# V rows of three token blocks: read in table order and multiplied with matrices of one-hot products, instead of gathered

## What is computed

```python
def block(xblk):                                   # 128 tokens
    q = (xblk @ w_q).reshape(PEER_BLOCK, PEER_HEADS, 2, PEER_HALF)
    s = jnp.einsum('thcd,hcnd->thcn', q, sub_keys).astype(jnp.float32)
    sv, si = lax.top_k(s, PEER_TOPK)
    ...
    expert = jnp.take_along_axis(cidx, pos, axis=-1)          # 8 heads x 16 of 16384 experts per token
    g = jax.nn.softmax(top_s, axis=-1)
    u = u_table[expert]
    hid = jax.nn.gelu(jnp.einsum('thkd,td->thk', u, xblk).astype(jnp.float32), approximate=False)
    v = v_table[expert]
    return jnp.einsum('thk,thkd->td', (g * hid).astype(xblk.dtype), v)
```

## Time and profile before

| | us |
|---|---|
| three runs, median (lowest to highest) | 3677.02 (3660.54 to 3686.26) |
| profiled execution | 3657.85 |
| its span, first to last instruction | 3655.7 |

### The profile page before, as it was taken

The page is one execution under the profiler, slowest core; times in us unless marked ns, Lnnn a source line. Parts: engine busy times, 40 slices in busy tenths (PEclk is TensorE's granted clock), DMA queues, the critical chain, the costliest instruction groups (busy, mean ns, idle before and its releaser), DMA issues.

```text
span 3655.7 us, 27703 instructions
## 1 busy us (share of the span) xinstructions
PE 1964.2 (54%) x9448; PEld 1078.6 (30%) x9448; DVE 2036.2 (56%) x4571; ACT 323.3 (9%) x778; POOL 2092.7 (57%) x2183
## 2 busy tenths in 40 slices
PE   6975553765763348655833367566633233333446
PEld 6765431543540125333601034233301000000001
DVE  2379747567548773664377843654586744443220
ACT  2211011011100010110100011101000000000000
POOL 0045523656557675566466765665576666666665
PEclk9985786976886669767866579678855655656569
DMA  6587965998999999999999999999999999999998
GB/s 224 179 308 282 398 224 184 385 398 342 387 396 360 364 358 394 402 351 401 340 388 361 356 375 394 396 363 395 358 359 368 359 374 366 367 371 376 372 371 324
DMA packets 442170, 1286.15 MB, mean 352 GB/s; under 512 B 39408, under 2 KB 157936, under 8 KB 442032
## 3 DMA queue, kind: packets, MB, share of 16 engines
q0 software_dynamic: 313344, 1140.99, 81.9%
q1 hardware_dynamic: 126224, 134.48, 11.0%
q10 hardware_dynamic: 2464, 8.91, 0.6%
HBM read 1274.50 MB, written 9.44 MB: 351 GB/s over the span
## 4 chain that ended last, share of the span: by engine, by line
POOL 24%; PE 17%; DMA 17%; issue 16%; DVE 15%; another core or an unknown queue 9%; ACT 1%; SPq 0%; POOLq 0%; ACTq 0%; DVEq 0%
POOL ring L631 24%; PE ps L1257 11%; DMA ring<-in_peer_v_dram,v_idx 9%; DVE ring L899 6%; PE ps L1216 4%; DMA ring<-in_peer_u_dram,u_idx 4%; DVE work L976 2%; DMA wbuf<-in_peer_w_q_dram 2%; DMA wbuf<-in_w_in_dram 1%; DVE work L972 1%; PE ps L1224 1%; DVE work L981 1%; DVE work L1073 1%; PE ps L1415 0%
## 5 line engine op out<-in xcount | busy, mean ns | idle before, releaser
L899 DVE CUSTOM_DVE_ANT_0 ring<-ring,ps 128x1024 f32<-128x1024 f32 x1088 | 1300.3, 1217 | 943.9 <-DMA ring<-in_peer_u_dram,u_idx 798.5
L631 POOL DMA_INDIRECT ring<-in_peer_u_dram,u_idx x1088 | 1037.7, 954 | 991.8 <-issue 275.7
L1216 PE MATMUL ps<-ring,spread 128*32 128x512 f32 x4352 | 874.5, 906 | 1231.0 <-DMA ring<-in_peer_v_dram,v_idx 1080.0
L631 POOL DMA_INDIRECT ring<-in_peer_v_dram,v_idx x1088 | 1053.2, 968 | 552.1 <-issue 303.5
L1257 PE MATMUL ps<-wbuf,actT 128*128 128x256 f32 (+1 forms) x2944 | 708.2, 400 | 111.6 <-issue 75.8
L1216 PEld LDWEIGHTS ps<-ring,spread 128*32 128x32 f32 x4352 | 177.8, 143 | 1821.8 <-issue 1759.8
L1257 PEld LDWEIGHTS ps<-wbuf,actT 128*128 128x128 f32 (+1 forms) x2944 | 560.2, 194 | 282.0 <-issue 182.3
L972 DVE MAX8 work<-work 128x8 f32<-128x128 f32 (+3 forms) x432 | 109.8, 322 | 60.0 <-ACT work L868 56.8
L976 DVE FIND_INDEX8 work<-work 128x8 uint32<-128x128 f32 (+3 forms) x432 | 134.0, 329 | 6.7 <-issue 6.7
L701 ACT COPY spread<-weightT 128x16 f32<-128x16 f32 x64 | 14.0, 219 | 878.3 <-remote 654.1
L899 DVE DVE_READ_ACCUMULATOR2_ANT hidden<- 128x1 f32 x1088 | 88.9, 82 | 0.0
(11 more groups left out here) (153 smaller groups left out, 1271.2 us busy)
## 6 DMA issues: line engine op xcount, KB each, us to landing
wbuf<-in_w_in_dram SPq DMA_DIRECT2D x55, 1024.0 KB
wbuf<-in_peer_w_q_dram SPq DMA_DIRECT2D x40, 1024.0 KB
wbuf<-in_w_out_dram SPq DMA_DIRECT2D x20, 1024.0 KB
ring<-in_peer_u_dram,u_idx POOLq DMA_INDIRECT x1088
ring<-in_peer_v_dram,v_idx POOLq DMA_INDIRECT x1088
x_v<-x_scratch ACTq DMA_DIRECT2D x8, 512.0 KB
out_dram<-x_v ACTq DMA_DIRECT2D x8, 512.0 KB
x_in<-in_x_prompt_dram SPq DMA_DIRECT2D x7, 512.0 KB
```

Of the source, the lines that this page charges most:

```text
L631: pool.indirect_dma_start(ring[:, at % RING, :], None, table, bass.IndirectOffsetOnAxis(ap=idx, axis=0)).then_inc(landed[at % RING], 16)
L899: ch.put(v_.tensor_tensor_reduce(out=row, in0=row, in1=ux_ps, scale=1.0, scalar=0.0, op0=ALU.mult, op1=ALU.add, accum_out=hidden[:, k:k + ...
L1216: mm = pe.matmul(ps[j:j + 32, B_ACC + c, :], spread[:, at:at + 32], tile[:, 512 * c:512 * c + 512], start=(t % 32 == 0), stop=(t % 32 == 3 ...
```

## The change

- `DENSE = [3, 4, 5]`: the V rows of these blocks are no longer gathered. 384 gathers of 512 KB leave the phases 2, 3 and 4, and `PHASES` cuts the remaining V work anew, so that block 1's ends in phase 3 and block 2's in phase 4. Phase 5 keeps its 192 u and 320 v.
- In phase 5, V is read once in table order: 128 tiles ("dense"), each 2 x 512 columns of 128 x 2 rows, 512 KB, by plain DMAs from SP into the same ring. An expert's number is 128 i1 + i2. The tiles go through four sessions (half of the i2 values, half of the columns).
- For each half of i2, a matrix `denseW` (128 i1 values x 64 i2 values x 384 tokens) is built ahead of its sessions: for four tokens at a time ("group", 96 per half), DVE writes one-hot rows of i1 (one `tensor_tensor` of 512) and of i2 times the weight (four `tensor_scalar` of 64), PE multiplies them (four matmuls of 64 columns), ACT copies the product out. Two buffers each.
- A dense tile then takes six matmuls of 128 x 128 by 512 columns (2 values of i2, 3 blocks). Sessions end in a copy or an addition of three 128 x 512 sums ("spill"), and blocks 3, 4 and 5 get their final norm after the last dense tile.
- `beside` spreads the dense items over phase 5's list: about 0.94 gathers after each build group, about 2.3 after each dense tile. After the last dense tile 35 v items of the sample are left.
- The ring has 13 places instead of 14; `weightT` has six buffers; the mixing stage's buffers share one tensor with `denseW`. The `x1` load of a final norm is its own item.

The order of items gives these numbers of gathers per stretch (u+v, by `Pace`; "rest" of a phase counted with `peer`):

| stretch | phase 2 before | phases 3, 4 before | phases 2, 3 after | phase 4 after |
|---|---|---|---|---|
| first norm and `w_in` | 54+24 | 48+40 | 48+20 | 39+16 |
| attention and retention | 66+32 | 55+56 | 53+28 | 43+24 |
| `w_out` and second norm | 20+13 | 25+32 | 27+16 | 46+24 |
| `w_q` | 24+26 | 23+16 | 20+8 | 0+0 |
| `peer` and rest | 92+97 | 105+112 | 108+56 | 128+0 |

In phase 5 after: build of half 0 with 48+43 gathers, sessions 0 and 1 with 75+73, build of half 1 with 34+56, sessions 2 and 3 with 35+84 and 29 of the sample, then 35 of the sample.

The core of the diff:

```diff
-RING = 14
+RING = 13
+DENSE = [3, 4, 5]
...
-    ([3, 4], [(1, 0, 64, 128), (2, 1)]),
-    ([5, 6], [(3, 2), (4, 3)]),
-    ([7, 8], [(5, 4), (6, 5)]),
+    ([3, 4], [(1, 0, 64, 128), (2, 1, 0, 64)]),
+    ([5, 6], [(3, 1, 64, 128), (4, 2, 0, 64)]),
+    ([7, 8], [(5, 2, 64, 128), (6, None)]),
...
+SESSIONS = [(0, 0), (0, 1), (1, 1), (1, 0)]
...
+    for n, (half, _) in enumerate(SESSIONS):
+        if n % 2 == 0:
+            items += [(0, ("oh", half, g)) for g in range(2)]
+            for g in range(GROUPS):
+                items.append((1.0, ("build", half, g)))
+                if g + 2 < GROUPS:
+                    items.append((0, ("oh", half, g + 2)))
+        items += [(2.45, ("dense", n, i)) for i in range(PAIRS)]
...
+                    sp.dma_start(ring[:, at % RING, :].rearrange("p (a n) -> p a n", a=2),
+                                 v_pairs[:, half * PAIRS + i, :, 512 * cols:512 * cols + 512]
+                                 ).then_inc(landing(at), 16)
...
+                act.wait_ge(built, n + 1)
+                src = ps[:, B_W[n % 2], 0:GROUP * I2].rearrange("p (t i) -> p i t", t=GROUP)
+                ch.put(copy(denseW[:, :, GROUP * g:GROUP * g + GROUP], src), w_copied)
...
+                if n >= 2:
+                    dve.wait_ge(built, n - 1)
+                t0, shape = GROUP * g, [P, GROUP, P]
+                ch.put(v_.tensor_tensor(one1[:, n % 2], iota.unsqueeze(1).broadcast_to(shape),
+                                        digit[:, 0, t0:t0 + GROUP].unsqueeze(2).broadcast_to(shape), ALU.is_equal))
+                for i in range(GROUP):
+                    t = t0 + i
+                    w = weightT[:, DENSE[t // P] % WTBUF, t % P:t % P + 1]
+                    ch.put(v_.tensor_scalar(one2[:, n % 2, i, :], iota[:, I2 * half:I2 * half + I2],
+                                            digit[:, 1, t:t + 1], w, ALU.is_equal, ALU.mult),
+                           ones_ready if i == GROUP - 1 else None)
...
+                for i in range(GROUP):
+                    mm = pe.matmul(ps[:, B_W[n % 2], i * I2:i * I2 + I2], one1[:, n % 2, i, :], one2[:, n % 2, i, :],
+                                   start=True, stop=True)
+                mm.then_inc(built, 1)
...
+                tile = await_tile(pe, "d", n * PAIRS + i)
+                for a in range(2):
+                    for j in range(len(DENSE)):
+                        mm = pe.matmul(ps[:, j, :], denseW[:, 2 * i + a, P * j:P * j + P],
+                                       tile[:, 512 * a:512 * a + 512], start=(i == 0 and a == 0),
+                                       stop=(i == PAIRS - 1 and a == 1))
```

More of the change, by code:

```diff
@@ L81, in u_before @@
     return SLOTS * b
+DENSE = [3, 4, 5]
+V_AT = {b: i for i, b in enumerate(b for b in range(NBLK) if b not in DENSE)}
 def v_before(b):
-    return P * b
+    return P * V_AT[b]
 def v_token(b, i):
@@ L161, in seg_items, with dense_items, beside @@
     return items
+GROUP = 4
+GROUPS = P * len(DENSE) // GROUP
+I2 = NKEY // 2
+PAIRS = I2 // 2
+SESSIONS = [(0, 0), (0, 1), (1, 1), (1, 0)]
+DENSE_SLOTS = PAIRS * len(SESSIONS)
+def dense_items():
+    items = [(0, ("digits", 0, 0))]
+    for n, (half, _) in enumerate(SESSIONS):
[6 more added lines that the diff above has]
+        items += [(2.45, ("dense", n, i)) for i in range(PAIRS)]
+        if n < 3:
+            items.append((0, ("spill", n, 0)))
+    for b in DENSE:
+        items += [(0, ("x1", b, 0)), (0, ("final", b, 0))]
+    return items
+def beside(items, others):
+    share = 0.93 * sum(kind in "uv" for kind, _, _ in items) / sum(n for n, _ in others)
+    out, seen, due, at = [], 0, 0.0, 0
+    for item in items:
+        while at < len(others) and due <= seen:
+            out.append(others[at][1])
+            due += others[at][0] * share
+            at += 1
+        out.append(item)
+        seen += item[0] in "uv"
+    return out + [item for _, item in others[at:]]
 def plan():
@@ L173, in plan @@
         out.append(items)
-    out[-1].append(("final", prev[1], 0))
+    out[-1] = beside(out[-1], dense_items()) + [("final", prev[1], 0)]
     return out
 PLAN = plan()
+ENDS = [b for items in PLAN for kind, b, _ in items if kind == "final"]
+assert ENDS == [b for items in PLAN for kind, b, _ in items if kind == "x1"] and len(ENDS) == NBLK
+END_AT = {b: n for n, b in enumerate(ENDS)}
 def gather_order():
@@ L188, in gather_order @@
                 order["v", v_before(b) + k] = len(order)
+            elif kind == "dense":
+                order["d", b * PAIRS + k] = len(order)
     return order
@@ L404, in hymba_peer_program @@
         landed = [sem(f"landed{i}") for i in range(RING)]
+        landed_d = [sem(f"landed_d{i}") for i in range(RING)]
         y_stored = sem("y_stored")
@@ L699, in spread_out @@
                 if v != SAMPLE:
-                    src = weightT[:].rearrange("p (j r) -> p r j", j=groups)[:, piece * runs:(piece + 1) * runs, :]
+                    src = weightT[:, v % WTBUF, :].rearrange("p (j r) -> p r j", j=groups)[:, piece * runs:(piece + 1) * runs, :]
                     ch.put(copy(dst, src), spread_ready)
@@ L888, in item @@
                     weights(b)
+                elif kind == "digits":
+                    digits()
+                elif kind == "spill" and b == 2:
+                    dve.wait_ge(dense_done, PAIRS * 3)
+                    dve.wait_ge(spilled, 2 * len(DENSE))
+                    for j in range(len(DENSE)):
+                        half = dense_sum[:, j, 512:1024]
+                        ch.put(v_.tensor_tensor(half, half, ps[:, j, :], ALU.add), spilled)
+                elif kind == "oh":
+                    one_hot(b, k)
                 elif kind == "final":
@@ L1200, in item @@
                     quad(b, k // QUAD)
+                elif kind == "build":
+                    build(b * GROUPS + k)
+                elif kind == "dense":
+                    dense(b, k)
                 elif kind == "weights":
```

193 lines of the change are left out of this document (137 added, 56 removed).

## The result

The change made the kernel slower: 3902.52 us in the median of four runs (3897.36 to 3907.49), against 3668.79 for the kernel before (four runs); the ratio is 1.062 with a 95% interval of 1.059 to 1.066. The profiled execution took 3897.73 us, its span 3895.3, and the forecast on that basis was 3715: 183 us too little. The forecast's direction held, its range (3640 to 3850) did not.

The account below looks back on a forecast made before the run. Transfers were taken to bound the kernel from 636 us on, PE the sessions after the change. 3657.85 - 387 (phases 2 to 4) + 444 (phase 5) = 3715 us, 3734 on the median; range 3640 to 3850.

Parts of the forecast that it names:

- Sessions: Phase 5, dense tiles: PE takes over as the bound at its full clock, 775 us, against 595 of transfers.
- Rival 2: Phase 5 sessions: long matmuls go faster, sessions at the transfers' 595 us, program 3554 us on the median; chance 0.05.
- Tail: End of phase 5: three chained final norms, then the sample's last strip, norm and store, 62 us (50 to 80).
- the change of phase: Phase 5: the change of phase, plus weights and final norms ACT must do between build copies, 8 us.
- Builds: Phase 5, building `denseW`: 1.85 us per group, 1.75 in half 1, 346 us together (300 to 425).
- the price of `tensor_scalar`: Builds, DVE: each of four 64-element operations per group taken at 0.12 us, so 1.09 per group with the 512-element one.
- the clock: Builds, PE: a PE busy 66% of its time had a clock of 0.80, used for the 1.85 us per group.
- Rival 3: Phase 5: PE's clock is low, builds 67 us more, sessions some 75; 3850 us on the median; chance 0.15.
- Phases 2 to 4: Removing 384 gathers (528 us of transfers) shortens these phases by 70, 173 and 144 us, together -387.
- attention: Attention stage of phases 2 and 3: 118 us each, between 111 of transfers and 125, from a chain over three engines.
- Rival 4: Phases 2 to 4: held by chains over all engines, only -300 us; 3821 on the median; chance 0.1.
- rival 1: Phases 2 to 4: give all their bare sums allow, -461 us; 3660 on the median, no change; chance 0.25.

Follow-up runs that it names:

- e8: Changed kernel with four instead of six matmuls per dense tile (block 5's sum left incomplete): 3534.83 us, ratio 1.037 to the kernel before.
- e6: Changed kernel with all gathers, dot products and quads moved from beside the builds to beside the sessions: 3668.74 us, ratio 1.076 to the kernel before.
- e15: Changed kernel with U and V tiles of phase 5 taken one by one in turn, not in bunches of four: 3717.95 us, ratio 1.090.
- e12: Changed kernel with one-hot rows from two 256-element operations and an unused 256-column matmul per build group: 3715.2 us, ratio 1.088.
- e16: Changed kernel with U and V in turn, one-hot rows from two 256-element operations, and an unused 256-column matmul per build group: 3665.37 us, ratio 1.075.
- e7: Changed kernel with DVE placing its dot products a quarter into each `peer` step, not a tenth: 3736.7 us, ratio 1.096 to the kernel before.
- e9: Changed kernel with two dense blocks instead of three, block 3's V rows gathered again: 3710.09 us, ratio 1.013 to the kernel before.
- a0: Changed kernel with three dense blocks, unaltered, run again as an anchor: 3885.13 us, ratio 1.060 to the kernel before.
- e10: Changed kernel with two dense blocks, only V gathers beside the builds and only U beside the sessions: 3649.46 us, ratio 0.997.
- e5: Changed kernel with only V gathers beside the builds, U beside the sessions, and an unused 256-column matmul per build group: 3614.02 us, ratio 1.060.
- e4: Changed kernel with only V gathers beside the builds and U gathers beside the sessions: 3855.43 us, ratio 1.056 to the kernel before.
- e3: Changed kernel with an unused 256-column filler matmul ahead of each build group: 3900.32 us, ratio 1.069 to the kernel before.
- e13: Two dense blocks, V beside builds, U beside sessions, one-hot rows from two 256-element operations, unused 256-column matmul per build group: 3438.6 us, ratio 1.009.
- e11: Changed kernel with one-hot rows from two 256-element operations in place of four `tensor_scalar`: 3733.77 us, ratio 1.095 to the kernel before.

## Why the forecast missed

- **Sessions (775, measured 771).** Right, and by the reason given: e8 shows PE as the bound. Rival 2 is out: a dense half takes 0.44 us. The estimate of 0.26 us from the 131 ns of the Trainium skill, "TensorE: Matmul & The Clock Gate", Back-to-back issue gap, does not hold for these fp32 matmuls; the formula of the same section, with two passes per half, gives an estimate of 0.43 us, which the trace agrees with.
- **Tail (62, measured 64)** and the change of phase (8, measured 6): right, and by the reason given. The third final norm ended 38 us after the last dense tile (37 forecast).
- **Builds (346, measured 472): the step that failed**, 126 of the 183 us, beyond its own bound of 425. The prediction took 1.85 and 1.75 us per group; the profile has 2.44 and 2.48. Three terms of it:
  - the price of `tensor_scalar`. The row it was taken from has immediates; with two scalars per partition it costs 0.22 us. 192 x 4 x 0.10 = 77 us more of DVE. That and half a dot per group give 2.07 and 1.90 us, 381 us in all.
  - the clock. The text took the 0.80 of a PE busy two thirds of its time; it was 0.59 to 0.61 though PE was busy 81 to 83%, and 0.50 in e6 at 100%. Rival 3 had the clock, with +67 us, and expected it in the sessions too, where it was 0.99 to 1.00.
  - the sum per group was of *mean* loads, but the loads come in bunches (e15 alone: 22 us). With the other two mended, breaking up the bunches gives 46 us (445 to 400, e12 to e16). The three together give 68 of the 126 us, and a good part of the rest is the price that the cheaper one-hot still has.
- **Phases 2 to 4 (-387, measured -325).** Against the working, w_in of phase 2 took 120 us (129), attention 135 (118), `w_out` to `w_q` 142 (135), `peer` 252 (240); phase 3 is 19 us over its sum and phase 4 16. In attention the prediction took the engines' chain for the later one; but in e7, at the faster pace, the same stage took 115 us at a DMA share of 1.02, here 135 at 0.92, with the same 101 to 103 us of DVE. It goes with the pace, though by more (15%) than the kernel before as a whole (7%), and what holds it at the slower pace is open. In `peer` DVE is at 225 of 252 us and the DMA share at 0.93: two loads, both near full, that don't overlap fully; e7 excludes DVE's placement as the cause, and what the last 10% are is open. Rival 4 (-300) was nearer than the forecast, rival 1 (-461) is out.
- **Sums of the prediction that do not come out.** The most that phases 2 to 4 could give is -434 by the two terms that it names (`peer` at DVE's bare sum, attention at its transfers), not -461; and the middle of both terms of rival 3 is 3734 + 71 = 3805 us on the median, not 3850. Neither enters the sum of the forecast; 3850 stands as the upper end of its range too.

## What to carry to other kernels

Where two engines hand work over through few buffers and each also serves a list of other items, don't sum mean loads: walk the list and add up the later engine of each bunch. Take an operation's price only from a row with the same operand kinds, or keep a range that holds twice that price. And before work is moved from the transfers to TensorE, count its columns at the measured rate: three blocks made TensorE the bound of the sessions by 200 us, two did not (e8, e9). The size of the shift was worth 175 us here (a0 to e9), the order of the rest 61 more (e9 to e10).

## What the hardware showed beyond that

- Two paces of the transfers for the same program: the kernel before took 3637 to 3671 us in two of the sets and 3402 to 3416 in three. The record gives the same chip number for sets 3 and 4, which had different paces, so the pace is not put down to the chip; what sets it is open, and as the kernel before has no profile at the faster pace, so is whether all its phases are shorter by one factor. In phases bound by them, the changed kernel moved 347 GB/s at a DMA share of 0.92 in attention at the slow pace, 409 at 1.02 at the fast one (e7); its builds and sessions took the same time in both (371 and 400 us). The attention of phase 2 in e7:

```profile
703.00:818.00 115.00, 74.86 (x423) 52.10 (x423) 101.04 (x177) 27.27 (x70) 81.50 (x85) 0.73 1.02 409
```

  A change that takes transfers out is therefore worth less at the fast pace: the changed kernel's ratio is 1.06 at the slow one, and 1.096 in e7, which differs from it in one placement only.
- TensorE's clock stayed at its lower level through 175 us in which the trace shows it busy without a pause, when all it had were 64-column matmuls (e6), and was 0.97 when each group had a 256-column matmul more, with quads in between (e5). That extra work shortens a stage (by 18%, e4 to e5) was not in the forecast; it paid only where nothing else held the builds (e5 yes; e3 and e13 no; beside the cheaper one-hot, e11 to e12, 21 us).
